# A new opening, low weight parts made ahead of time, and split products for the differential scores

## The reference, cut to what matters

```python
mod_l = jnp.split(s_lat @ ada_w[i] + ada_b[i], ADA_CHUNKS, axis=-1)   # s_lat = silu(c), s_ctx = silu(c_ctx)
h_lat = modulate(x_lat, mod_l[0], mod_l[1])      # rms_norm(x) * (1 + scale) + shift
q, k, v, g = jnp.split(h @ w_in, splits, axis=-1)                     # retention; g is the gate projection
...
s = jnp.einsum('bqhmd,bkhmd->bhmqk', q, k).astype(jnp.float32) * scale   # 8 heads x 2 maps of 64 features
p = jax.nn.softmax(s, axis=-1); p = p[:, :, 0] - lam * p[:, :, 1]
...
a = u @ w_pw1 + b_pw1; a = a[..., :CONV_DIM] * jax.nn.sigmoid(a[..., CONV_DIM:])
a = dwconv(a, w_dw)                              # depthwise, 31 taps; latents in rows of 64
a = jax.nn.silu(layer_norm(a + b_dw, ln_g, ln_b)); y = a @ w_pw2 + b_pw2
```

## Time and profile before

| | us |
|---|---|
| median of the 3 runs (2 lie at 3006.3 and 3006.4, one at 3010.8) | 3006.41 |
| the profiled execution, its own time | 3006.21 |
| its span, from the first to the last instruction | 3004.4 |
| TensorE busy | 2949.9 |
| VectorE, ScalarE, GpSimd busy | 2129.7, 1192.7, 193.5 |

### The profile page before, as it was taken

One profiled execution on the slowest core, in us unless ns is written; L12 is line 12 of the kernel. 1 busy time (PEld: TensorE's weight loads), 2 busy tenths in 40 slices (PEclk: granted clock), 3 DMA queues, 4 the chain that ended last, 5 costly groups with the idle time before them and its releaser, 6 DMA issues.

```text
span 3004.4 us, 40234 instructions
## 1 busy us (share of the span) xinstructions
PE 2949.9 (98%) x14353; PEld 2420.3 (81%) x14353; DVE 2129.7 (71%) x3282; ACT 1192.7 (40%) x1803; POOL 193.5 (6%) x163
## 2 busy tenths in 40 slices
PE   7999999999999999999999999999999999999998
PEld 5888678888887789977888888788888888876787
DVE  6973688877786788699898876566754632756875
ACT  3223524332143664556441323443244422423443
POOL 2300000000001000000040210000000000002120
PEclk9999999999999999999999999999999999999999
DMA  7672065666633156311266552672366622452554
GB/s 276 200 245 92 21 197 174 215 202 240 205 102 112 57 182 222 129 57 43 99 208 212 175 183 76 213 248 100 102 219 215 215 91 92 150 188 95 199 186 144
DMA packets 125230, 479.26 MB, mean 160 GB/s; under 512 B 13752, under 2 KB 13752, under 8 KB 122768
## 3 DMA queue, kind: packets, MB, share of 16 engines
q1 hardware_dynamic: 119232, 443.60, 44.5%
q0 software_dynamic: 5840, 33.51, 3.1%
HBM read 459.23 MB, written 17.83 MB: 159 GB/s over the span
## 4 chain that ended last, share of the span: by engine, by line
PE 79%; issue 10%; DVE 6%; ACT 2%; DMA 1%; SPq 0%; POOL 0%; DVEq 0%; ACTq 0%; POOLq 0%
PE bank L798 21%; PE bank L800 21%; PE bank L799 21%; PE bank L811 4%; PE bank L812 2%; PE bank L1727 2%; PE bank L1100 1%; DVE x_res L2667 1%; DVE w_lo L2551 1%; PE bank L810 1%; DMA ada_first<-in_ada 1%; DVE x_res L2673 1%; PE bank L1206 1%; ACT w_hi L1795 1%; DMA ml_v<-v_spill 0%
## 5 line engine op out<-in xcount | busy, mean ns | idle before, releaser
L2551 DVE TENSOR_TENSOR w_lo<-w_raw,w_hi 128x1024 fp32r<-128x1024 f32 x617 | 754.7, 1231 | 498.1 <-ACT w_hi L1795 489.1
L1795 ACT ACTIVATE w_hi<-w_raw 128x1024 fp32r<-128x1024 f32 x620 | 649.5, 1055 | 755.6 <-PE bank L800 626.4
L798 PE MATMUL bank<-h_hi,w_hi 128*128 128x512 f32 (+1 forms) x1432 | 524.5, 366 | 7.3 <-DVE h_lo L2640 5.2
L799 PE MATMUL bank<-h_lo,w_hi 128*128 128x512 f32 (+1 forms) x1432 | 518.9, 362 | 0.0
L800 PE MATMUL bank<-h_hi,w_lo 128*128 128x512 f32 (+1 forms) x1432 | 518.8, 362 | 0.0
L798 PEld LDWEIGHTS bank<-h_hi,w_hi 128*128 128x128 f32 x1432 | 270.4, 189 | 54.9 <-issue 9.7
L799 PEld LDWEIGHTS bank<-h_lo,w_hi 128*128 128x128 f32 x1432 | 270.4, 189 | 43.7 <-issue 1.2
L800 PEld LDWEIGHTS bank<-h_hi,w_lo 128*128 128x128 f32 x1432 | 270.3, 189 | 41.6
L798 PE MATMUL bank<-w_hi,xm_hi 128*128 128x512 f32 x512 | 201.0, 393 | 0.1
L800 PE MATMUL bank<-w_hi,xm_lo 128*128 128x512 f32 x512 | 199.4, 389 | 0.0
L799 PE MATMUL bank<-w_lo,xm_hi 128*128 128x512 f32 x512 | 199.3, 389 | 0.0
(11 more groups left out here) (473 smaller groups left out, 5667.3 us busy)
## 6 DMA issues: line engine op xcount, KB each, us to landing
w_raw<-in_weights SPq DMA_DIRECT2D x620, 512.0 KB, 4.2
ada_ring_f<-in_ada SPq DMA_DIRECT2D x56, 512.0 KB, 3.4
ada_ring_g<-in_ada SPq DMA_DIRECT2D x44, 512.0 KB, 3.4
ada_ring_b<-in_ada SPq DMA_DIRECT2D x38, 512.0 KB, 4.2
ada_ring_a<-in_ada SPq DMA_DIRECT2D x32, 512.0 KB, 3.4
ada_first<-in_ada SPq DMA_DIRECT2D x16, 512.0 KB, 15.3
v_spill<-ml_v POOLq DMA_DIRECT2D x4, 1024.0 KB, 6.9
o_spill<-ml_o_grp POOLq DMA_DIRECT2D x4, 1024.0 KB, 4.6
```

The source lines that it names most:

```text
L798: mm(out, lhs[0], rhs[0], start=start, stop=False)
L799: mm(out, lhs[0], rhs[1], start=False, stop=False)
L1795: return nc.scalar.activation(out, in_, func, **kw)
L2551: V.tensor_tensor(WLO[:, slot, :], RAW[:, slot, :], WHI[:, slot, :].bitcast(F32), SUB)\
```

## The change

- Opening: one row of c and c_ctx on one partition (8 KB) and one row of ones are loaded in place of the spread rows; TensorE spreads them into four banks with one-row matmuls, ScalarE takes the Silu out of the banks. The projection weights are queued behind all modulation weights, the loads of tiles 4 to 6 behind the first loads of the next modulation weights. All eight squares have buffers of their own; TensorE takes their sums in pairs between its modulation tiles. VectorE inverts the root after its last product, and makes the first three low weight parts in eight slices between the modulation steps; GpSimd makes none. Five turn-over matmuls stand ahead of the projection.
- In the gate projection 14 later weight tiles (pointwise tiles 5 to 15 and the first three after them) are loaded by GpSimd's queue, split by ScalarE and VectorE, and their low parts stored to DRAM. The buffers lie on `x_res`, which is loaded again afterwards. In the convolution GpSimd's queue loads these low parts in place of VectorE's subtractions.
- `PE_TAPS` is 14, six times 8, 15, so VectorE has 21 taps in the middle chunks instead of 19.
- Scores: q and k are split into high parts (ScalarE) and low parts (VectorE, in place), and each step is six split matmuls of 64 rows.

```diff
-PE_TAPS = [14] + [10] * 6 + [15]
+PE_TAPS = [14] + [8] * 6 + [15]
+N_SPLIT = 14
...
-            sp.dma_start(C_ROWS[:, 0:2, :], c_rows_d[:, 0:2, :]).then_inc(S("c_rows_in"), 16)
+            sp.dma_start(C_ROW, c_rows_d[0:1, 0:2, :]).then_inc(S("c_rows_in"), 16)
+            sp.dma_start(ONE_ROW, consts_d[1][0:1, :]).then_inc(S("c_rows_in"), 16)
             for n in range(ADA_FIRST):
...
-                if n == 9:
-                    for s in range(LOOKAHEAD):
-                        sp.dma_start(RAW[:, s, :], weights[s]).then_inc(raw_full[s], 16)
+            for s in range(SLOTS):
+                sp.dma_start(RAW[:, s, :], weights[s]).then_inc(raw_full[s], 16)
...
+            for i in range(N_SPLIT):
+                pool.wait_ge(S("split_lo"), N("split_lo", i + 1))
+                pool.dma_start(lo_spill[i], SLO[:, i % 2, :]).then_inc(S("split_out"), 16)
+                pool.wait_ge(S("split_out"), N("split_out", 16 * (i + 1)))
+                if i + 2 < N_SPLIT:
+                    split_load(i + 2)
+            pool.dma_start(X[:, :, :], x_t).then_inc(S("x_again"), 16)
...
+            for i in range(N_SPLIT):
+                n = split0 + i
+                pool.wait_ge(S("tile_done"), n - LOOKAHEAD)
+                pool.dma_start(WLO[:, n % SLOTS, :], lo_spill[i]).then_inc(S("lo_in"), 16)
+                pool.wait_ge(S("w_hi_done"), n + 1)
+                pool.wait_ge(S("lo_in"), N("lo_in", 16 * (i + 1)))
+                pool.sem_inc(S("w_lo_done"), 1)
...
+            for b in range(4):
+                mm(PS[1 + b][:, :], ONE_ROW, C_ROW[:, b // 2, b % 2 * 512:b % 2 * 512 + 512], start=True, stop=True)\
+                    .then_inc(S("c_spread"), 1)
...
+                if n >= 7:
+                    for c in {7: (0, 1), 9: (2, 3), 11: (4, 5), 13: (6, 7), 15: ()}[n]:
+                        pe.wait_ge(S("sq_done"), c + 1)
+                        mm(PS[0][:, :], ONES[:, :], FIRST_SQ[:, c, :], start=c == 0, stop=c == DC - 1)\
+                            .then_inc(S("sq_used"), 1)
...
+            turn_over(5, 6)
...
+                for i in range(3):
+                    for m in range(2):
+                        part = slice(64 * m, 64 * (m + 1))
+                        q = (DQLO if i == 2 else DQHI)[part, h, t * P:(t + 1) * P]
+                        k = (DKLO if i == 1 else DKHI)[part, h, :]
+                        last = mm(PS[D_SCORE[u % 2][m]][:, :], q, k, start=i == 0, stop=i == 2)
...
+            def first_low(k):
+                cols = slice(k * P, (k + 1) * P)
+                if k == 0:
+                    dve.wait_ge(S("w_hi_done"), LOOKAHEAD)
+                last = V.tensor_tensor(WLO[:, 0:LOOKAHEAD, cols], RAW[:, 0:LOOKAHEAD, cols],
+                                       WHI[:, 0:LOOKAHEAD, cols].bitcast(F32), SUB)
...
-                if p:
-                    lo_ahead("pw1", t - 1, t - 1)
-                if 0 < p < DC - 1:
-                    lo_ahead("pw1", t, t)
```

More of the change, by code:

```diff
@@ L611, in _ @@
                 load_ada(slot, slot, AREA_A)
+            for n in range(SLOTS, SLOTS + LOOKAHEAD):
+                sp.wait_ge(S("w_lo_done"), n + 1 - SLOTS)
+                sp.dma_start(RAW[:, n % SLOTS, :], weights[n]).then_inc(raw_full[n % SLOTS], 16)
             load_phase("ret_qk", 16, 0, AREA_A, goes_on=True)
@@ L961, in gemm_rows @@
                 for s in range(ahead):
-                    if half is None:
+                    if half is None and not lows_by_chunk:
                         pe.wait_ge(S("w_lo_done"), g0 + s + 1)
@@ L1203, in d_scores @@
                     pe.wait_ge(S("d_exp"), 2 * (u - 1))
-                for m in range(2):
-                    part = slice(64 * m, 64 * (m + 1))
-                    mm(PS[D_SCORE[u % 2][m]][:, :], DQ[part, h, t * P:(t + 1) * P], DK[part, h, :],
-                       start=True, stop=True).then_inc(S("d_score"), 1)
+                if t == 0:
+                    pe.wait_ge(S("d_lo_done"), N("d_lo_done", 4 + h + 1))
+                for i in range(3):
[4 more added lines that the diff above has]
+                        last = mm(PS[D_SCORE[u % 2][m]][:, :], q, k, start=i == 0, stop=i == 2)
+                        if i == 2:
+                            last.then_inc(S("d_score"), 1)
             def first_scores(k):
@@ L2107, in d_copies, with q_high, k_high @@
                     f(dst, PS[D_BANKS[g][b]][:, :], ACT.Copy).then_inc(S("dtok_copy"), 1)
+            def q_high():
+                for b in range(4):
+                    f(q_pair(DQHI, b), q_pair(DQ, b), ACT.Copy).then_inc(S("d_hi_done"), 1)
+            def k_high(heads):
+                for h in heads:
+                    f(DKHI[:, h, :], DK[:, h, :], ACT.Copy).then_inc(S("d_hi_done"), 1)
             def v_copies(g):
@@ L2130, in _ @@
                 d_copies(g)
+                if g == 0:
+                    act.wait_ge(S("dtok_copy"), 4)
+                    q_high()
+            act.wait_ge(S("dtok_copy"), 12)
+            k_high(range(4))
             v_copies(3)
@@ L2173, in do_high @@
                   scale=DCOL[:, 1:2]).then_inc(S("do_hi_done"), 1)
-            for n in range(22, 26):
+            for n in range(22, 25):
                 d_high(n)
+            k_high(range(4, DIFF_HEADS))
+            d_high(25)
             d_exps(0)
@@ L3125, in _ @@
                 d_low(12 + 4 * g)
+                if g == 1:
+                    q_low()
+            k_low(range(1))
             v_copies(3)
+            k_low(range(1, 3))
             d_low(21)
@@ L3169, in d_head_rstd @@
                 own(V.reciprocal(D_RSTD[:, cols], D_VAR[:, cols]))
-            for n in range(23, 26):
-                d_low(n)
+            d_low(23)
+            d_low(24)
+            k_low(range(4, DIFF_HEADS))
+            d_low(25)
             for u in range(2):
```

137 lines of the change are left out of this document (93 added, 44 removed).

## The result

The changed kernel takes 3019.3 us (median of 20 runs, 3007.0 to 3023.1), the kernel before 3006.6 (20 runs). The ratio over all runs is 1.003 (95% interval 1.0022 to 1.0037); the two medians give 1.004, since a median lies in one of the groups described next. I had forecast 2992 and a range of 2984 to 3005. The 20 times are two groups: 7 from 3007.0 to 3009.8, 13 from 3016.3 to 3023.1. The profiled execution (3022.0, span 3020.2) is of the upper one. Two executions of later kernels (3266.7 in experiment 9, 3255.2 in experiment 12) had a mean granted clock of 0.85 where all others had 0.99 or more, and are left out of their kernels' medians and ranges.

The account below looks back on a forecast made before the run. TensorE, busy 98% of the span, was taken to bound the kernel. Opening -8.5, convolution -2.6 and scores -3 sum to -14.1, from the median 3006.41 to 2992.1 us; range 2984 to 3005.

Parts of the forecast that it names:

- The gate projection: Low parts made there hide behind TensorE; the two-deep ring's round takes 10.5 us within two tiles' 10.9, cost 0.
- rival 5: Gate projection's two-deep ring is late once store and reload together pass 12.4 us: 3012 and up; chance 0.05.
- The row of 3.3: Gate projection: SyncE's weights land in 3.3 us, the low end of 3.3 to 4.6 for each ring transfer.
- The retention: Stage held for unchanged; if it moves by more than 1 us, the prediction is wrong as a whole.
- The opening: Earlier loads and a clock that rises after one slow pair and tile: -8.5 us, ends -11 and +4.
- the slow one: Opening's clock stays at 1.2 GHz: opening +4, total 3004; chance 0.18.
- The scores: Differential scores: six split matmuls save 0.2 us a step, times 16, -3 us; ends -5 and +5.
- The convolution: TensorE loses 12 taps, VectorE becomes the bound: -2.6 us, ends -8.3 and -2.
- The pitch: Convolution: VectorE's time per chunk stays 18.36 us.
- the exposed 0.97: Convolution: VectorE's idle of 0.97 us before the low part in chunk 0, expected where covering subtractions are removed.
- chunk 7's start: Convolution: chunk 7 starts at 1385.8 instead of 1388.04.
- the removed subtractions of the last chunk give 0.3 more: Convolution, last chunk: removing VectorE's subtractions gains a further 0.3 us.

Follow-up runs that it names:

- experiment 9: Changed kernel without gate-projection splits and with the old convolution taps, sums of squares as three, two, two, one between modulation tiles: 2995.1 us, ratio 0.9957.
- experiment 12: Changed kernel with three ring buffers, load issued before the store wait, sums as four, two, one, one, and 13 taps in the last chunk: 2993.8 us.
- Experiments 3 and 4: Changed kernel with three ring buffers: 3 issues the next load before waiting for the store, 3005.93 us; 4 waits for each store first, 3006.4 us.
- experiment 5: Changed kernel without storing low parts in the gate projection; the convolution loads the same volume from the weights instead: 2992.2 us.
- Experiment 10: Changed kernel with three ring buffers, load issued before the store wait, eight sums in a row, 13 instead of 15 taps in the last chunk: 2996.1 us.

## Why the prediction was wrong, by its own steps

**The gate projection was the step that failed** ("taken 10.5, cost 0"). The round's parts were right in kind, and rival 5 named what queues behind a late load. What failed is the size of the transfers. I took each between 3.3 and 4.6 us, and 8.2 for the two. In the round above the load took 4.5, the store 5.7, and copy and subtraction 2.6 for 2.3: 12.7 instead of 10.5. That is 0.9 a tile over TensorE's pace, and the offset grew by 0.8 a tile. The row of 3.3 has no other transfer beside it, but that is not the whole of it: the 1 MB stores behind the 4.6 ran beside weight loads too (DMA share 0.72 to 0.82) and were twice as large. Why half a megabyte took longer here stays open.

The sum also had no term for GpSimd, which does nothing between a store and its landing: two issues of 0.5 us and a store of 5.0 are 6.1 us a tile by themselves, over TensorE's 5.44. Experiments 3 and 4 show that both the depth of the ring and GpSimd's waiting count.

And the sum left out that ScalarE splits, evacuates and makes high parts of three tiles at once at the start of the stage, so that five transfers fall together: one store takes 10.4 us from issue to landing, and the offset grows by 9.8. That the bunch makes this store late is argued from the trace; the same bunch took 6.7 and 8.0 us for its store with three buffers (experiments 3 and 4), and what keeps one or two DMA engines behind with two buffers is open. That all of it comes with the store is shown by experiment 5.

Rival 5 named the outcome (3012 and up, 3019.3 measured). It put the point where this decides at 12.4 for store and load; they were 10.1 in steady state, and it decided all the same, since the bunch came on top. Its chance of 0.05 was far too small for a ring with 0.4 us to spare. The retention, named in the prediction as a stage whose change would make it wrong as a whole, did change: its first products wait 7.88 us for 0.71. The Trainium skill ("DMA: Bandwidth & Descriptors", section "Latency and other measured facts") says that two of the sixteen DMA engines are usually slower than the others when GpSimd issues. That fits the last landing here, where one engine's share of traffic is all that is left for 3.5 us; no run of this case shows which engine it was, or why.

**The opening.** The mechanism and both sizes were right: 8.5 gained was forecast for the early clock and 9.7 to 10.4 measured where it holds at least to the last tile, +4 for the slow one and +2.5 to +2.9 measured. (A pair at 1.2 GHz was priced at 3.3 and took 3.55: the 0.76 us a record were five records in a window of 3.8, while their starts lie 0.85 apart.) What failed is to treat the two as cases of which one is true of the kernel. Each execution goes one way or the other: of the profiles with pairs first, three are slow throughout and three fast. In the changed kernel 17 of 30 times are in the upper group. With three or more sums first (seven profiles) the clock rose each time, between 3 and 6 us after the first of them by the length of the rows. The Trainium skill ("TensorE: Matmul & The Clock Gate", section "HAM oscillation") has the clock fall in the waits between bursts; here it stayed up through single tiles of two columns between wide sums, and fell under three and five such tiles in a row, in some executions under two, and once in the last single sum (experiment 12), without any wait.

**The scores**: -1.8 to -2.0 for -3. The matmuls came out nearly as priced (0.89 us for 0.85, 0.17 off for 0.2). The term that was too large is the step: it saves 0.11, not 0.2. VectorE and ScalarE are at 22.2 and 22.6 of 25.4 us, and in every second step ScalarE's two small copies come ahead of what TensorE needs. I argue this from the timeline, no run tested it.

**The convolution**: -1.4 for -2.6. The pitch (18.35 for 18.36), the exposed 0.97 and chunk 7's start were right. The term "the removed subtractions of the last chunk give 0.3 more" was not: with them gone, TensorE's 15 taps end last there, and 2.7 us of waiting come back. Experiment 10 shows it by taking two of them away.

**The sum.** Had the execution been of the early kind, the change would still have been at about 3007: -9.7 + 14 - 1.9 - 1.4. The gains of the scores and the convolution were there in either case, that of the opening only with the early clock. The ring ate them, and the clock decided between no change and 0.4% slower.

## What to carry to other kernels

A ring must be sized with the duration that its transfers have when all of them run at once, and the stage's start is where they do: this one had 4% to spare on paper and did not fit. The engine that issues the transfers and waits for each is a ring of its own and needs its own sum. When a kernel's times fall into two groups, look for the group first and for the cause second; a profile shows one execution of one of them, and an order of matmuls that makes the clock rise each time can be worth more than the work that it hides. When one engine's load is lightened in the middle of a loop, look at the last turn as well, which may still be balanced for the old load.

## What was not expected of the hardware

- With pairs of wide sums between two-column tiles, TensorE's clock rose in three of six profiled executions, 2.8 to 3.3 us after the first sum, with the same instructions before it and the first sum at 18.5 to 18.8 us in all six. It is worth some 12 us.
- The 512 KB store of GpSimd took 5.0 us (median) beside loads of 4.2, and 10.0 to 10.4 in the bunch in all three profiles with two buffers, where one or two DMA engines were still at work 3.4 us after the rest. The DMA engines were busy 0.80 of the time for 233 GB/s there; in the kernel before, where the same bunch (244 to 250 us) has weight loads alone, 0.74 for 251, and in the opening 1.01 for 421. Stores alone do not explain the difference: in experiment 3 the bunch, with its store, had 1.01 for 354 (238 to 244 us).
- Two matmuls on different halves of the rows, with split operands, cost 0.30 us together in the mean of three pairs, and 0.23 in the middle one, which is what one of 128 rows costs; as float32 one pair was 1.06 for its four records.
